# Full attention on one Trainium2 core: the product of weights and values in three one-pass products, and a query tile's maxima over both key halves at once

## The chip, the cores and the metric

One core of one Trainium2 chip runs the whole program. The metric is the time of one execution on the device, in microseconds (us); smaller is better. The program is written engine by engine: TensorE (PE; its weight loads are PEld), VectorE (DVE), ScalarE (ACT), GpSimd (POOL) and SyncE (SP) each run their own list of instructions in order, and semaphores tie them together.

## The reference, cut to what matters

The program is two transformer blocks. The change is in the attention of the first: 8 query heads and 2 key/value heads of width 64, over 1024 tokens, with no mask.

```
q, k, v = heads(q_a), heads(k_a), heads(v_a)      # 8, 2, 2 heads of 64
q = rope(rms_norm(q)); k = rope(rms_norm(k))
for each block of 128 queries:
    s = einsum('bkgqd,bksd->bkgqs', q, k) * 64 ** -0.5
    p = softmax(s, axis=-1)
    o = einsum('bkgqs,bksd->bkgqd', p, v)
```

All of it is in float32. The rest (projections, the bidirectional mLSTM, the feed-forward part, the second block with its banded and its forgetting attention) isn't touched.

## The kernel before, in words

A `Plan` lists steps; each engine then walks the same list and does its own part of every step. The order of that list is therefore the order on every engine. `attention` (L160) writes it for one kind of attention; "full" is the kind that the change touches.

**Jobs and units.** A job is one head and one half of the queries (512 queries): 16 jobs, numbered here 0 to 15. A job has 8 units, one for each tile of 128 keys. For unit g the plan puts down, in this order: the scores of the unit after it (`sc`); steps that are due (`mrow`, `take`, `div`, `qhi`, `qlo`); a unit of maxima for a later job (`max`); now and then a portion of other work for TensorE, `share` of one for each unit (9 matmuls, about, of the input projection, L1216 to L1218, or steps that prepare the mLSTM); and last the values of unit g (`val`).

**Scores.** `scores` (L1342, L1344) makes scores of 128 keys by 512 queries with keys along the partitions, in one of two PSUM banks (2 and 3). Each operand is split into a rounded part (type fp32r, which TensorE takes in one pass) and a low part (what the rounding left), so that two one-pass matmuls give the float32 product. The second of them (L1344) also subtracts the maximum of each query, through one extra row of `qa`.

**Weights and values.** ScalarE takes the exponential of the bank into `pf` (L1829, 128x512, float32), one of three buffers. `values` (L1366) multiplies `pf` by the values, both plain float32, into bank 6 or 7, where a job's 8 units add up. The stationary operand is 128 columns wide: 64 of values and 64 of ones, so rows 64 to 127 of the result hold the sums of the weights. A float32 matmul stands in the trace as two records. After a job's last unit `take` makes the reciprocals of the sums on ScalarE (a logarithm, L1837, and an exponential, L1839), and `divide` multiplies on VectorE (L2154, `y<-ps,rinv`).

**Maxima.** They have to be known before a job's first scores. `max_unit` computes one tile of 128 queries against one half of the keys (L1307, one matmul of 128x512), and VectorE takes the maximum of each row of the bank (L2290, 128x512). A job has 8 such units: 4 query tiles, 2 halves. VectorE then takes the larger of the two halves for all four tiles (`mx<-mh`, 128x4), four small matmuls with an identity turn the four columns into a row (`mrow`, L1323), and ScalarE copies that row into `qa` (L1809), which releases the semaphore `row`.

**The helper banks.** Banks 4 and 5 serve `max`, `mrow`, the turned values (`vprep`) and the turned gates, each step taking the other one than the step ahead of it. A step waits until the step two places before it has been emptied (`aux_emptied`): by VectorE's reduction (semaphore `aux`), or by ScalarE's copy of the row (`row`).

**Before the first scores** the plan has the maxima of job 0 and the first of job 1, two units of maxima and then a portion of projection matmuls in turn.

Of the kernel before, what the change touches and what calls it, by code (L numbers as in the profile page):

```python
# [15 lines left out]
P = 128  # L16
D = 1024
T = 1024
# [61 lines left out]
for _name, _n in (("b_ada", 48), ("b_ada_2", 24), ("norm_mix_g", 8), ("norm_ffn_g", 8),  # L80
# [16 lines left out]
    "half_mm y_out pad_made conv_taps conv_out m_kept m_in o_in rope_in qk_sq side_mm side_out qk_r qk_n qk_swap qk_cos qk_sin qk_rot "  # L97

    "at_set vt aux kk_hi kk_cp kk_lo q_hi q_cp q_lo mx_mm mcol rowt row sink_f sink_h sink_l sink_mm "
    "sc p_exp val ln_r inv div "  # L100
# [52 lines left out]
def max_units_of(kind, h, n):  # L153

    if kind == "band":
        return [(4 * n, None), (4 * n + 2, None)]
    return [(qt, half) for qt in range(4 * n, 4 * n + 4) for half in range(2) if kind == "full" or half <= n]


def attention(p, jobs, fill, share, at):  # L160
# [42 lines left out]
    for g, (i, u) in enumerate(units):  # L203
# [12 lines left out]
        if u == len(units_of(*job)) - 1:  # L216
            waiting.append(("take", *job))
# [492 lines left out]
def build(nc, a, out):  # L710
# [3 lines left out]
    with ExitStack() as ctx:  # L714
# [103 lines left out]
        class Buffers:  # L818
            def __init__(self, n, k_area, v_area, q_area, p_area):
# [4 lines left out]
                self.v = [v_area[i](f"{n}_v{i}", [P, KT, P], F32) for i in range(2)]  # L824
# [6 lines left out]
        A1 = Buffers("full", four(64, 72, 80, 88), four(68, 136), area, (76, 92, 144))  # L831
        A1.mx = [area(f"mx1_{i}", [P, 4], F32R) for i in range(3)]
        A1.mh = [area(f"mh1_{i}", [P, 2, 4], F32) for i in range(3)]
        area = Area(148, 152)
        A1.rinv = [area(f"rinv1_{i}", [64, HT], F32) for i in range(2)]
# [194 lines left out]

        def aux_bank(*step):
            return 4 + AUX_NO[step] % 2
# [5 lines left out]
        def aux_emptied(step):  # L1038

            i = AUX_NO[step] - 2  # L1040
            if i < 0:
                return None
            if AUX[i][0] == "gate":
                return s["g_cols"], G_COLS[AUX[i][1]]
            return (s["row"], no(*AUX[i])) if AUX[i][0] == "mrow" else (s["aux"], aux_no(*AUX[i]))
# [167 lines left out]
        def tensor(e):  # L1213
# [51 lines left out]
            def aux_free(step):  # L1265
                if emptied := aux_emptied(step):
                    e.wait_ge(*emptied)
# [9 lines left out]
            def max_unit(kind, h, n, u):  # L1277
# [26 lines left out]
                else:  # L1304
                    k0, k1 = half * HT, min((half + 1) * HT, T if kind == "full" else (qt + 1) * P)
                    if kind == "full":
                        x = e.matmul(ps[:, bank, 0:k1 - k0], q(qt), A.kk[kb][:, k0:k1], start=True, stop=True, skip_group_check=True)  # L1307
                    else:
# [1803 lines left out]
```

## Time and profile before

| what | value |
|---|---|
| median of 3 runs | 1998.36 us (1997.38 to 2002.4) |
| span of the profiled execution | 1999.4 us |
| TensorE busy in it | 1928.1 us (96%) |
| full attention, first scores to last values | about 278 to 519 us |
| granted TensorE clock there | 1.00 (of 2.4 GHz) |

The profile is one execution on the chip. A span of it is the time from its first instruction to its last; no other time of that execution is given, so the span stands for it. Busy times are unions of an engine's records. A record of ScalarE or VectorE can begin before the one ahead of it has ended, and so can TensorE's, whose ends are modelled; the distance from start to start is what an instruction costs in a dense stretch. "<-" behind an idle time names what ended it.

### The profile page before, as it was taken

How to read it: one execution, taken by the hardware profiler on the slowest of the kernel's cores; microseconds unless marked ns; L12 is line 12 of the kernel's file. 1: busy time of each engine (PE TensorE's matmuls, PEld its weight loads, DVE VectorE, ACT ScalarE, POOL GpSimd, SP SyncE). 2: the span in 40 equal slices, each digit the busy share in tenths (PEclk: the TensorE clock that was granted, in tenths of full speed). 3: DMA queues.
4: the chain of work that ended last, by engine and by line, in shares of the span. 5: the costliest groups of instructions: out<-in, count | busy, mean ns of one | idle time of the engine just before them, and what ended most of it. 6: DMA issues, size and time to landing. Idle time of an engine off the chain costs nothing.

```text
span 1999.4 us, 23686 instructions
## 1 busy us (share of the span) xinstructions
PE 1928.1 (96%) x8844; PEld 1507.4 (75%) x8844; DVE 1209.4 (60%) x1774; ACT 909.3 (45%) x1523; POOL 104.6 (5%) x188
## 2 busy tenths in 40 slices
PE   6999999999989989999999999999999999999888
PEld 4778876656787768888888788887888887776577
DVE  7794847655575687677555546556543555445744
ACT  5543345465553542333333435434523665445742
POOL 1101100000000000111000000000021000000000
PEclk9999999999999999999999999999999999999999
DMA  8437400010205423355221653333432001013062
GB/s 325 161 95 241 165 25 11 1 53 1 95 1 167 160 95 121 138 184 200 68 70 53 219 202 121 120 127 138 158 126 74 33 32 43 22 56 146 1 179 95
DMA packets 67151, 216.13 MB, mean 108 GB/s; under 512 B 8272, under 2 KB 13520, under 8 KB 66784
## 3 DMA queue, kind: packets, MB, share of 16 engines
q1 hardware_dynamic: 47168, 141.15, 21.1%
q0 software_dynamic: 19872, 73.48, 10.4%
q8 instruction: 72, 1.18, 0.2%
q14 instruction: 39, 0.32, 0.1%
HBM read 177.30 MB, written 34.61 MB: 106 GB/s over the span
## 4 chain that ended last, share of the span: by engine, by line
PE 57%; DVE 4%; ACT 2%; DMA 2%; issue 1%; DVEq 0%; SPq 0%; ACTq 0%
PE ps L1216 9%; PE ps L1218 8%; PE ps L1217 8%; PE ps L1522 6%; PE ps L1523 6%; PE ps L1524 6%; PE ps L1366 4%; DMA w_raw<-in_weights 2%; PE ps L1342 1%; PE ps L1344 1%; PE ps L1310 1%; DVE w_lo L2158 1%; PE ps L1652 1%; PE ps L1651 1%; PE ps L1650 1%
## 5 line engine op out<-in xcount | busy, mean ns | idle before, releaser
L1216 PE MATMUL ps<-h_hi,w_hi 128*128 128x512 f32 x832 | 335.5, 403 | 7.5 <-DVE h_lo L2158 5.2
L1218 PE MATMUL ps<-h_hi,w_lo 128*128 128x512 f32 x832 | 326.4, 392 | 0.0
L1217 PE MATMUL ps<-h_lo,w_hi 128*128 128x512 f32 x832 | 326.1, 392 | 0.0
L2158 DVE TENSOR_TENSOR w_lo<-w_raw,w_hi 128x1024 fp32r<-128x1024 f32 x139 | 170.0, 1224 | 244.0 <-ACT w_hi L1689 242.6
L1689 ACT ACTIVATE w_hi<-w_raw 128x1024 fp32r<-128x1024 f32 x140 | 147.6, 1056 | 243.6 <-DMA w_raw<-in_weights 241.8
L2290 DVE TENSOR_REDUCE mh<-ps 128x1 f32<-128x512 f32 (+1 forms) x224 | 140.2, 630 | 142.1 <-PE ps L1307 68.0
L1216 PEld LDWEIGHTS ps<-h_hi,w_hi 128*128 128x128 f32 x832 | 158.1, 190 | 43.1 <-DVE h_lo L2158 6.4
L1218 PEld LDWEIGHTS ps<-h_hi,w_lo 128*128 128x128 f32 x832 | 157.3, 189 | 34.1
L1217 PEld LDWEIGHTS ps<-h_lo,w_hi 128*128 128x128 f32 x832 | 157.7, 190 | 32.1 <-issue 1.4
L1216 PE MATMUL ps<-hid_hi,w_hi 128*128 128x512 f32 x352 | 138.1, 392 | 4.1 <-DVE hid_kept_lo L2158 1.9
L1522 PE MATMUL ps<-t_hi,pair_S_r 128*128 128x512 f32 x352 | 137.3, 390 | 4.4 <-DVE pair_S_r L2158 2.6
L1218 PE MATMUL ps<-hid_hi,w_lo 128*128 128x512 f32 x352 | 137.1, 389 | 0.0
L1524 PE MATMUL ps<-t_hi,pair_S_r 128*128 128x512 f32 x352 | 137.0, 389 | 0.0
L1523 PE MATMUL ps<-t_lo,pair_S_r 128*128 128x512 f32 x352 | 137.0, 389 | 0.0
L1366 PE MATMUL ps<-full_pf,full_v 128*128 128x512 f32 x256 | 131.0, 593 | 0.3 <-ACT full_pf L1829 0.2
L1829 ACT ACTIVATE second_pf<-ps 128x512 f32<-128x512 f32 (+2 forms) x128 | 65.1, 510 | 136.6 <-PE ps L1348 61.3
L1829 ACT ACTIVATE full_pf<-ps 128x512 f32<-128x512 f32 x128 | 76.1, 596 | 98.1 <-PE ps L1344 97.5
L1366 PE MATMUL ps<-second_pf,second_v 128*128 128x128 f32 (+3 forms) x336 | 111.8, 434 | 0.8 <-ACT second_pf L1829 0.7
L1342 PE MATMUL ps<-full_qq,full_kk 128*128 128x512 f32 x128 | 90.4, 706 | 0.2 <-issue 0.2
L1216 PE MATMUL ps<-mix_hi,w_hi 128*128 128x512 f32 x192 | 77.2, 402 | 8.8 <-ACT y_out L2121 6.1
L1342 PE MATMUL ps<-second_qq,second_kk 128*128 128x128 f32 (+3 forms) x168 | 83.5, 497 | 1.7 <-ACT second_pf L1829 0.7
L1216 PEld LDWEIGHTS ps<-hid_hi,w_hi 128*128 128x128 f32 x352 | 66.1, 188 | 20.5 <-DVE w_lo L2158 2.9
(405 smaller groups left out, 3829.9 us busy)
## 6 DMA issues: line engine op xcount, KB each, us to landing
w_raw<-in_weights SPq DMA_DIRECT2D x140, 512.0 KB, 3.6
ada_next<-in_ada POOLq DMA_DIRECT2D x32, 512.0 KB, 4.8
ada_last<-in_ada POOLq DMA_DIRECT2D x24, 512.0 KB, 5.2
pair_gate<-in_weights SPq DMA_DIRECT2D x22, 512.0 KB, 3.7
pair_up<-in_weights SPq DMA_DIRECT2D x22, 512.0 KB, 4.6
ada_first<-in_ada SPq DMA_DIRECT2D x8, 1024.0 KB, 17.7
m_scratch<-y POOLq DMA_DIRECT2D x12, 512.0 KB, 5.5
hid_scratch<-hid_out POOLq DMA_DIRECT2D x22, 256.0 KB, 2.3
```

The lines of the kernel that those rows point to most:

```text
L1216: e.matmul(o, w_hi[slot][:, tile_of(kw)], hi, start=start, stop=False, skip_group_check=skip)
L1217: e.matmul(o, w_hi[slot][:, tile_of(kw)], lo, start=False, stop=False, skip_group_check=skip)
L1218: return e.matmul(o, w_lo[slot][:, tile_of(kw)], hi, start=False, stop=stop, skip_group_check=skip)
L1342: e.matmul(o, A.kk[kb][:, keys], A.qq[b][:, q], start=True, stop=False, skip_group_check=True)
L1366: x = e.matmul(o, A.v[kb][:, kt, :], A.pf[p3][:, c:c + q1 - q0], start=(u == 0 and kind != "band"), stop=False, skip_group_check=True)
L1522: e.matmul(ps[:, bank, :], a_hi[:, tile_of(k)], b_hi[:, first + k, :], start=start and k == 0, stop=False, skip_group_check=True)
L1523: e.matmul(ps[:, bank, :], a_hi[:, tile_of(k)], b_lo[:, first + k, :], start=False, stop=False, skip_group_check=True)
L1524: x = e.matmul(ps[:, bank, :], a_lo[:, tile_of(k)], b_hi[:, first + k, :], start=False, stop=k == 3, skip_group_check=True)
L1689: return e.activation(dst, src, ACT.Copy)
L1829: e.activation(A.pf[p3][:, c0:c1], ps[:, bank, c0:c1], ACT.Exp, scale=SC).then_inc(s["p_exp"], 1)
L2158: return e.tensor_tensor(dst, src, hi.bitcast(F32), ALU.subtract)
L2290: x = e.tensor_reduce(A.mh[b][:, half, i:i + 1], ps[:, bank, 0:k1 - k0], AX_X, ALU.max)
```

## The change

For the full attention alone:

- **Weights times values.** ScalarE takes the exponential of a score bank twice: into `p_hi` (rounded, fp32r) and into `pf` (float32). VectorE subtracts one from the other into `p_lo` (step `plo`, in the place of `pf`). The values are split once for each key/value head into `v_hi` and `v_lo`. `values` is then `v_hi*p_hi` and `v_lo*p_hi` (the second with 64 stationary columns, since the ones have no low part), and a new step `vlo`, one unit later, adds `v_hi*p_lo`. The product of the two low parts is left out. `take` comes one unit later than before, and there is one `rinv` buffer where there were two.
- **Maxima.** A unit of maxima is a query tile against all 1024 keys: two matmuls into banks 4 and 5, then one reduction over 128x1024 straight into `mx`. A job has 4 such units; from job 3 on they stand at every other unit of the plan. VectorE's combination of halves is gone, and `mrow` on TensorE waits for the reductions themselves. A maxima step waits until both banks have been emptied.
- Semaphores of the rotary part are joined into one (`qk_step`) with the same order of instructions.

```diff
@@ max_units_of
+    if kind == "full":
+        return [(qt, None) for qt in range(4 * n, 4 * n + 4)]
@@ attention
-        low = max(first[i - 2], high - len(maxima) + 1) if i >= 3 else high - len(maxima) + 1
+        span = 2 * len(maxima) if jobs[i][0] == "full" and i >= 3 else len(maxima)
+        low = max(first[i - 2], high - span + 1) if i >= 3 else high - span + 1
...
+        if job[0] == "full":
+            p.add("plo", *job, u)
         for step in rows + waiting + others + slots.get(g, []):
             p.add(*step)
...
         p.add("val", *job, u)
...
+        if job[0] == "full":
+            if g:
+                p.add("vlo", *jobs[units[g - 1][0]], units[g - 1][1])
@@ buffers
+        A1.rinv = [Area(148, 150)("rinv1", [64, HT], F32)] * 2
+        A1.p_hi = [Area(start, start + 2)(f"full_p_hi{i}", [P, HT], F32R) for i, start in enumerate((94, 146, 150))]
+        A1.p_lo = [Area(start, start + 2)(f"full_p_lo{i}", [P, HT], F32R) for i, start in enumerate((76, 92, 144))]
@@ helper banks
+            banks = (4, 5) if x[:2] == ("max", "full") else (4 + AUX_NO[x] % 2,)
@@ aux_emptied
-            i = AUX_NO[step] - 2
...
+            for b in AUX_BANKS[step]:
+                i = AUX_USED[b].index(step) - 1
@@ TensorE, max_unit
+                        for n1 in range(2):
+                            x = e.matmul(ps[:, 4 + n1, :], q(qt), A.kk[kb][:, half_of(n1)], start=True, stop=True, skip_group_check=True)
@@ TensorE, values and values_low
+                if kind == "full":
+                    e.matmul(ps[:, bank, :], A.v_hi[kb][:, u, :], A.p_hi[p3][:, :], start=u == 0, stop=False, skip_group_check=True)
+                    e.matmul(ps[0:64, bank, :], A.v_lo[kb][:, u, :], A.p_hi[p3][:, :], start=False, stop=False,
+                             skip_group_check=True).then_inc(s["val_hi"], 1)
+                    return
...
+                e.wait_ge(s["p_lo"], i)
+                e.matmul(ps[:, 6 + job_no(kind, h, n) % 2, :], A.v_hi[kb][:, u, :], A.p_lo[(i - 1) % 3][:, :], start=False,
+                         stop=False, skip_group_check=True).then_inc(s["val"], 1)
@@ ScalarE, scores
+                if kind == "full":
+                    if i > 3:
+                        e.wait_ge(s["val_hi"], i - 3)
+                        e.wait_ge(s["p_lo"], i - 3)
...
+                    e.activation(A.p_hi[p3][:, :], ps[:, bank, :], ACT.Exp, scale=SC).then_inc(s["p_hi"], 1)
@@ VectorE, max_unit
+                elif kind == "full":
+                    x = e.tensor_reduce(A.mx[b][:, i:i + 1], flat(4), AX_X, ALU.max)
@@ VectorE, p_low
+                e.wait_ge(s["p_exp"], i)
+                low_part(A.p_lo[p3][:, :], A.pf[p3][:, :], A.p_hi[p3][:, :]).then_inc(s["p_lo"], 1)
```

TensorE where one job hands over to the next but one (the row of job 10's maxima is turned, and the maxima of job 11 begin). `full_qq,full_kk` and `full_qa,full_ka` are the two matmuls of the scores, `full_kk,full_qq` the maxima, `ident_r,mx` the turned row. Before:

```order
L1344 MATMUL ps<-full_qa_142,full_ka_138 128x512
L1323 MATMUL ps<-ident_r,mx_1_151 1x128 [waits ident_made,mcol,aux]
L1323 MATMUL ps<-ident_r,mx_1_151 1x128 x3
L1307 MATMUL ps<-full_kk_136,full_qq_141 128x512 [waits q_cp,kk_lo,q_hi,aux]
L1366 MATMUL ps<-full_pf_147,full_v_146 128x512 [waits p_exp]
L1342 MATMUL ps<-full_qq_140,full_kk_136 128x512 [waits kk_lo,kk_cp,q_lo,at_set,row,p_exp]
L1344 MATMUL ps<-full_qa_143,full_ka_138 128x512
L1307 MATMUL ps<-full_kk_136,full_qq_141 128x512 [waits kk_lo,row]
```

And of the changed program:

```order
L1372 MATMUL ps<-full_qa_142,full_ka_138 128x512
L1351 MATMUL ps<-ident_r,mx_1_149 1x128 [waits ident_made,aux]
L1351 MATMUL ps<-ident_r,mx_1_149 1x128 x3
L1331 MATMUL ps<-full_kk_136,full_qq_141 128x512 [waits q_cp,kk_lo,q_hi,row,aux]
L1331 MATMUL ps<-full_kk_136,full_qq_141 128x512
L1393 MATMUL ps<-full_p_hi_152,full_v_hi_159 128x512 [waits p_hi]
L1394 MATMUL ps<-full_p_hi_152,full_v_lo_161 64x512
L1406 MATMUL ps<-full_p_lo_157,full_v_hi_159 128x512 [waits p_lo]
L1370 MATMUL ps<-full_qq_140,full_kk_136 128x512 [waits kk_lo,kk_cp,q_lo,at_set,row,p_exp]
```

The wait for `row` stood at the scores after the values (L1342) and now stands at the maxima right behind the turned row (L1331), ahead of the values. The same pair stands so at the rows of jobs 2 to 14, 13 times.

ScalarE at the same kind of place, where the row is copied. In the changed program:

```order
L1876 ACTIVATE full_p_hi_154<-ps 128x512 [waits p_lo,val_hi,sc]
L1879 ACTIVATE full_pf_147<-ps 128x512 [waits val]
L1854 ACTIVATE full_qa_142<-ps 1x512 [waits sc,rowt]
L1876 ACTIVATE full_p_hi_152<-ps 128x512 [waits p_lo,val_hi,sc]
L1879 ACTIVATE full_pf_145<-ps 128x512 [waits val]
L1728 ACTIVATE full_qq_141<-y 64x512 [waits qk_rot,sc]
```

Ahead of the copy (L1854) stand two exponentials of the newest scores, where there was one (L1829).

## Rows read from the trace of the kernel before

**Rows 1.** The page, busy time of each engine over the span.

```profile
PE 1928.1 (96%) x8844; PEld 1507.4 (75%) x8844; DVE 1209.4 (60%) x1774; ACT 909.3 (45%) x1523; POOL 104.6 (5%) x188
```

**Rows 2.** Stretches of jobs 1 to 4, of job 4 alone, of job 8: us, busy by engine, clock.

```profile
297.50:359.83 62.33, 62.19 (x225) 39.57 (x223) 47.01 (x65) 34.62 (x58) 0.00 (x0) 1.00 0.03 9
343.31:359.83 16.52, 16.38 (x62) 10.57 (x60) 14.05 (x23) 10.65 (x18) 0.00 (x0) 1.00 0.00 0
405.28:418.24 12.96, 12.96 (x47) 7.68 (x45) 7.63 (x14) 7.21 (x13) 0.00 (x0) 1.00 0.53 201
```

**Rows 3.** Timeline of TensorE in the last job: start, us, engine, line, operation.

```profile
512.03 0.39 PE L1344 MATMUL ps<-full_qa,full_ka 65*128 65x512 f32 x1
512.26 1.02 PE L1366 MATMUL ps<-full_pf,full_v 128*128 128x512 f32 x2
...
513.35 0.40 PE L1344 MATMUL ps<-full_qa,full_ka 65*128 65x512 f32 x1
513.59 0.59 PE L1366 MATMUL ps<-full_pf,full_v 128*128 128x512 f32 x1
```

**Rows 4.** Groups by line and form, 275 to 522 us: count, busy, mean ns, idle before.

```profile
L2290 DVE TENSOR_REDUCE mh<-ps 128x1 f32<-128x512 f32 x120 | 82.2, 687 | 66.4 <-PE ps L1307 65.8
L1829 ACT ACTIVATE full_pf<-ps 128x512 f32<-128x512 f32 x128 | 76.1, 596 | 98.1 <-PE ps L1344 97.5
L1323 PE MATMUL ps<-ident_r,mx 128*1 128x128 f32 x64 | 6.5, 223 | 3.6 <-issue 2.4 <-DVE mh L2290 1.0
```

**Rows 5.** Timeline of all engines where job 8 hands over.

```profile
413.57 0.40 PE L1344 MATMUL ps<-full_qa,full_ka 65*128 65x512 f32 x1
413.81 0.40 PE L1323 MATMUL ps<-ident_r,mx 128*1 128x128 f32 x4
414.00 0.60 ACT L1829 ACTIVATE full_pf<-ps 128x512 f32<-128x512 f32 x1 [0.96 <-PE ps L1344]
414.05 0.44 PE L1307 MATMUL ps<-full_kk,full_qq 128*128 128x512 f32 x1
414.33 1.02 PE L1366 MATMUL ps<-full_pf,full_v 128*128 128x512 f32 x2
...
414.63 0.58 ACT L1809 ACTIVATE full_qa<-ps 1x512 fp32r<-1x512 f32 x1
...
415.28 0.19 PEld L1342 LDWEIGHTS ps<-full_qq,full_kk 128*128 128x128 f32 x1 [0.76 <-ACT full_pf L1829]
```

**Rows 6.** Timeline of ScalarE, two exponentials without a wait between.

```profile
434.89 1.06 ACT L1829 ACTIVATE full_pf<-ps 128x512 f32<-128x512 f32 x2
```

**Rows 7.** Timeline of ScalarE at a take.

```profile
431.22 0.59 ACT L1837 ACTIVATE rinv<-ps 64x512 f32<-64x512 f32 x1
431.84 0.63 ACT L1839 ACTIVATE rinv<-rinv 64x512 f32<-64x512 f32 x1
432.50 0.60 ACT L1829 ACTIVATE full_pf<-ps 128x512 f32<-128x512 f32 x1
```

**Rows 8.** Groups of VectorE by form, whole span.

```profile
L2158 DVE TENSOR_TENSOR w_lo<-w_raw,w_hi 128x1024 fp32r<-128x1024 f32 x139 | 170.0, 1224 | 244.0 <-ACT w_hi L1689 242.6
...
L2290 DVE TENSOR_REDUCE mh<-ps 128x1 f32<-128x384 f32 x16 | 8.9, 556 | 5.9 <-PE ps L1313 5.7
...
L2290 DVE TENSOR_REDUCE mh<-ps 128x1 f32<-128x128 f32 x16 | 4.7, 291 | 14.2 <-PE ps L1313 14.2
```

**Rows 9.** Timeline of projection matmuls, and of the first maxima.

```profile
257.04 0.39 PE L1216 MATMUL ps<-h_hi,w_hi 128*128 128x512 f32 x1
...
257.72 0.39 PE L1216 MATMUL ps<-h_hi,w_hi 128*128 128x512 f32 x1
...
264.52 0.61 PE L1307 MATMUL ps<-full_kk,full_qq 128*128 128x512 f32 x2
...
265.89 1.28 DVE L2290 TENSOR_REDUCE mh<-ps 128x1 f32<-128x512 f32 x2
```

More of the change, by code:

```diff
@@ L156, in max_units_of @@
         return [(4 * n, None), (4 * n + 2, None)]
-    return [(qt, half) for qt in range(4 * n, 4 * n + 4) for half in range(2) if kind == "full" or half <= n]
+    if kind == "full":
+        return [(qt, None) for qt in range(4 * n, 4 * n + 4)]
+    return [(qt, half) for qt in range(4 * n, 4 * n + 4) for half in range(2) if half <= n]
 def attention(p, jobs, fill, share, at):
@@ L215, in attention @@
         p.add("val", *job, u)
-        if u == len(units_of(*job)) - 1:
-            waiting.append(("take", *job))
+        ended = (g, i, u)
+        if job[0] == "full":
+            if g:
+                p.add("vlo", *jobs[units[g - 1][0]], units[g - 1][1])
+            if g == len(units) - 1:
+                p.add("vlo", *job, u)
+            else:
+                ended = (g - 1, *units[g - 1]) if g else None
+        if ended and ended[2] == len(units_of(*jobs[ended[1]])) - 1:
+            waiting.append(("take", *jobs[ended[1]]))
     while fill:
@@ L1029, in build @@
         AUX_NO = {x: i for i, x in enumerate(AUX)}
+        AUX_USED, AUX_BANKS = {4: [], 5: []}, {}
+        for x in AUX:
+            banks = (4, 5) if x[:2] == ("max", "full") else (4 + AUX_NO[x] % 2,)
+            AUX_BANKS[x] = banks
+            for b in banks:
+                AUX_USED[b].append(x)
         def aux_bank(*step):
-            return 4 + AUX_NO[step] % 2
+            return AUX_BANKS[step][0]
         def aux_no(*step):
@@ L1265, in aux_free @@
             def aux_free(step):
-                if emptied := aux_emptied(step):
+                for emptied in aux_emptied(step):
                     e.wait_ge(*emptied)
@@ L1304, in max_unit @@
                 else:
-                    k0, k1 = half * HT, min((half + 1) * HT, T if kind == "full" else (qt + 1) * P)
                     if kind == "full":
-                        x = e.matmul(ps[:, bank, 0:k1 - k0], q(qt), A.kk[kb][:, k0:k1], start=True, stop=True, skip_group_check=True)
+                        e.wait_ge(s["kk_lo"], no("klo", kind, kb, 1))
+                        for n1 in range(2):
+                            x = e.matmul(ps[:, 4 + n1, :], q(qt), A.kk[kb][:, half_of(n1)], start=True, stop=True, skip_group_check=True)
                     else:
+                        k0, k1 = half * HT, min((half + 1) * HT, (qt + 1) * P)
                         diagonal = k1 == (qt + 1) * P
@@ L1353, in values @@
                 p3, bank = (i - 1) % 3, 6 + job % 2
-                e.wait_ge(s["p_exp"], i)
+                e.wait_ge(*((s["p_hi"], i) if kind == "full" else (s["p_exp"], i)))
                 if u == 0:
@@ L1761, in head_squares @@
                 if r >= 2:
-                    e.wait_ge(s["qk_n"], r - 1)
+                    e.wait_ge(s["qk_step"], 4 * (r - 2) + 1)
                 e.wait_ge(s["y_out"], no("y1", t, 1))
@@ L1834, in take @@
                 e.wait_ge(s["val"], no("val", kind, h, n, last_unit((kind, h, n))))
-                if job >= 2:
-                    e.wait_ge(s["div"], job - 1)
-                e.activation(rinv[:, :], ps[64:P, bank, :], ACT.Ln).then_inc(s["ln_r"], 1)
-                e.wait_ge(s["ln_r"], job + 1)
+                if job >= 1:
+                    e.wait_ge(s["div"], job if kind == "full" else job - 1)
+                e.activation(rinv[:, :], ps[64:P, bank, :], ACT.Ln).then_inc(s["inv"], 1)
+                e.wait_ge(s["inv"], 2 * job + 1)
                 e.activation(rinv[:, :], rinv[:, :], ACT.Exp, scale=-1.0).then_inc(s["inv"], 1)
```

76 lines of the change are left out of this document (46 added, 30 removed).

## The prediction

> **What bounds the kernel now.** I read the page first, then busy time by stretch, then the timeline where jobs meet. TensorE is busy for 96% of the span, no other engine for more than 60% [rows 1]. The full attention says the same: in job 8, which has no other work mixed in, TensorE is busy for all 12.96 us, VectorE for 7.63, ScalarE for 7.21 [rows 2]. So what TensorE issues is paid in full, and the other two engines have some 5 us of room in a job. The question is how much of that room the change eats, and in which order the three now wait for each other.
>
> **Products of weights and values.** In the last job, without maxima, a unit takes 1.33 us (512.26 to 513.59), and the second score matmul takes 0.24 of it (513.35 to 513.59) [rows 3]. With two one-pass matmuls of about 0.235, the float32 product is left with 0.86 us. Three one-pass products at 0.235 take 0.705, which is 0.155 less, over 128 units 19.8 us. The nearest other price is the projection's pace, 0.68 us for three (257.04 to 257.72) [rows 9]; with it the gain would be 23. I take 0.235, since the new matmuls wait and signal as those of the scores do. The 64-column load isn't in the trace; nothing says that a shorter load shortens a pass by more than the projection's pace shows.
>
> For a 512-column matmul the Trainium skill (TensorE: Matmul & The Clock Gate, Back-to-back issue gap) gives 512/2.4 + 2.5, about 216 ns. The float32 product agrees (0.86 for four passes); the one-pass matmuls don't. By its figure alone the gain would be 27.6 us, an estimate.
>
> **The wait for the turned row, the largest new cost.** Maxima now take both helper banks. In the order of the changed program, 13 times (jobs 2 to 14), the pair of maxima stands right behind the turned row and waits until ScalarE has copied that row. Before, the maxima took the other bank and the value product (0.86 us) stood between; the wait was met almost exactly [rows 5]: second score matmul 413.57, turned row 413.81, free for the next at 414.05; the exponential begins at 414.00, 0.43 after 413.57; the copy at 414.63, 0.63 later; it ends at 415.21, and the next scores load at 415.28.
> In the changed order two exponentials stand ahead of the copy. A second one follows its like by 0.48 (1.06 less 0.58) [rows 6]. So the copy ends 0.43 + 0.48 + 0.63 + 0.58 = 2.12 after the second score matmul, the maxima start at about 2.17, and TensorE was ready at 0.48: **1.69 us idle, 13 times, 22.0 us**. Bounds: 20 if the copy too follows by 0.48, 24 if the exponentials are 0.62 apart. Behind the waiting pair stand the values of the unit, its low product, portions of projection and the next job's first scores, so nothing fills the hole. For the rows of jobs 1 and 15 no maxima follow; the next job's first scores wait, behind 0.7 us of products: together 1.5 us (0 to 2).
>
> The Trainium skill (Perfetto Trace Analysis, Matmuls) wants independent matmul groups to rotate through PSUM banks, so that one is emptied while the next is computed. The change gives that up for the maxima.
>
> **Waits that go.** TensorE's turned row used to wait for the last reduction and the combination of halves, 3.6 us in all [rows 4]; the last pair now stands two units ahead of it. The short wait there (the product of 414.33 would have let the scores start at 415.19; they start near 415.31) [rows 5] is replaced too, 15 times 0.12. Together -5.4 us (-3.6 to -5.4).
>
> **ScalarE.** It gains 128 exponentials of 0.60 us [rows 4], 0.48 apart at the least: 8 x 0.48 = 3.8 to 8 x 0.62 = 5.0 us a job on 7.2 busy [rows 2], in a job of some 13. That fits, except at the take: logarithm and exponential are 0.62 apart and the next exponential follows 0.66 later [rows 7]. Counted from the second score matmul of that unit, the next `p_hi` starts at 0.91 + 0.62 + 0.62 + 0.66 = 2.81 and is done at 3.41; TensorE, after 13 more passes of 0.235, wants it at 3.05. That is 0.4 us a job where no other work stands in that unit; I count 10 of 16 jobs, 4 us (0 to 7).
>
> **VectorE.** A job gains 8 subtractions, 0.60 us each when dense (128x512, by the pace of the reductions: 1.28 for two [rows 9]), 4.8 us. Its 8 reductions of 0.687 [rows 4] become 4 over 1024 columns. From 128 to 384 columns a reduction grows from 291 to 556 ns, 1.04 ns a column; that gives 687 + 530 = 1.22 us, as a 1024-column subtraction takes (1224 ns) [rows 8]. So -0.6, and 0.2 for the combination: **+4.0 us a job**. Job 8: 11.6 of 12.96 - 1.24 + 1.69 = 13.4, enough. Jobs 1 to 4, where the gates' scans run: 47.0 + 16 = 63.0 us of work against 62.3 - 5.0 + 3 x 1.69 + 1 = 63.4 of TensorE, waits included [rows 2]. Even on average, so bursts spill over: job 4 has 14.05 + 4.0 = 18.1 against 16.5 - 1.2 + 1.7 = 17.0. I take 3 us (0 to 8, if nothing is evened out and the mLSTM's preparation in jobs 11 to 15 is held up too). The waits for the row give VectorE time to catch up; without them this would be the bound.
>
> **Ahead of and behind the stage.** The plan begins with two pairs of maxima in a row. The second waits for the first reduction, which can't begin before 265.89 [rows 9]: idle from about 265.0 to 267.2. The fourth waits for the third likewise, about 1.3. Before, banks alternated, and about 1 us was lost there. Net +2.5 us (0 to 3.5). At the end the last low product waits for exponential, exponential, subtraction: +0.6 (0 to 1). The rotary semaphores move no instruction: 0, since each is waited for by the next on the same engine.
>
> **The sum.** -19.8 + 22.0 + 1.5 - 5.4 + 4 + 3 + 2.5 + 0.6 = +8.4 us. The profiled span is 1.0 above the median of the runs, so I add to the median: 1998.4 + 8.4 = **2006.8 us**. Later stages are bound by TensorE as well, and move by as much.
>
> **Rivals.**
> *The passes run faster and the other engines keep up* (the side of a gain). One mechanism: the new matmuls reach the projection's pace, which gives 3.3 us more, and projection work falls into the units of the takes and bursts, so the 4 and the 3 aren't paid. Then 2006.8 - 3.3 - 7 = 1996.5, and with the copy 0.48 behind the exponential (-1.8) and half of the start 1993.5. For it: the projection [rows 9]. Against: every one-pass matmul beside a semaphore in this stage is 0.235 apart. A gain beyond the noise begins where this and the lower bound of the row's wait come together. 11%.
> *The passes run at 0.216.* 0.019 us less for each of 384 products is 7.3 us: 1999.5, no change. The float32 passes do run at that pace [rows 3]; against it, no one-pass matmul here does. The Trainium skill (same page and section) would have it so. 12%.
> *ScalarE becomes the bound.* If both exponentials and what follows are 0.62 apart, a job asks for 16 x 0.62 + 2.5 = 12.4 us, and between the copied row and the next scores ScalarE is idle for 1.9: 14.3 against 13.8 with the take, and more in jobs with the mLSTM's work. 8 us more: 2015. The take [rows 7] speaks for 0.62, the pair of exponentials [rows 6] against. 12%.
> *The wait for the row doesn't bite*, because something fills it: excluded by TensorE's order, in which all behind the pair waits too. It would be 1985; 1%, within the first.
> The forecast has the remaining 65%.
>
> **Numbers.** A measurement of this kernel can tell about 0.3%, 6 us, from no change: 1992.4 and 2004.4 are the bounds. The forecast with its bounds lies above 2004.4 for some 52 of its 65%, within for 13. Slower: 52 + 12 = 64%. Same: 13 + 12 = 25%. Faster: 11%. All lower bounds together give 1990, all upper ones 2020; 8 times in 10 it should be between 1995 and 2016.
>
> **What would show it.** Right: 13 idle times of TensorE of about 1.7 us in the full attention, ended by ScalarE's copy of the row (L1854); three products of a unit in about 0.7 us; TensorE's busy time in the stage down by about 20 us and its idle time up by more; reductions of 1.2 us; VectorE near full in jobs 1 to 4. Wrong: idle times at the maxima under 1 us, products 0.65 us or 0.8 us a unit, idle times at `p_hi` or `p_lo` that outweigh those at the row, or a difference outside the stage (278 to 519 us now).

## The result, and the profile after

The changed kernel takes **2034.78 us**, the median of four runs (2033.52 to 2038.76), against 1999.77 for four runs of the kernel before beside them (1997.38 to 2002.4): a ratio of 1.0177, 95% interval 1.0161 to 1.0193. It is 35 us slower. The forecast was 2006.8 us, 8.4 more than before, with a range of 1995 to 2016. The sign was right, the size was not.

The page of the changed kernel, busy time over the span of 2033.4 us (beside [rows 1]):

```profile
PE 1919.2 (94%) x8972; PEld 1524.7 (75%) x8972; DVE 1276.7 (63%) x1822; ACT 970.5 (48%) x1653; POOL 104.2 (5%) x188
```

TensorE is busy for 8.9 us less and the span is 34.0 us longer, so TensorE waits. The stretches of jobs 1, 2, 4, 6, 7 and 8, from one take to the next (beside [rows 2]): start and end, length, then busy time of PE, PEld, DVE, ACT and POOL, and PE's granted clock.

```profile
302.09:322.21 20.12, 16.86 (x72) 11.67 (x70) 15.89 (x18) 12.26 (x22) 0.00 (x0) 1.00 0.00 1
322.21:343.03 20.82, 16.83 (x63) 12.18 (x63) 15.72 (x19) 10.88 (x21) 0.00 (x0) 0.84 0.00 0
...
360.22:381.33 21.11, 16.58 (x70) 11.49 (x69) 19.28 (x26) 15.51 (x27) 0.00 (x0) 1.00 0.00 0
...
397.91:421.18 23.27, 19.99 (x102) 14.62 (x101) 13.17 (x18) 13.13 (x26) 0.00 (x0) 1.00 0.00 1
421.18:439.00 17.82, 14.12 (x62) 10.24 (x61) 11.52 (x16) 12.47 (x24) 0.00 (x0) 0.90 0.02 3
439.00:452.95 13.95, 12.21 (x54) 8.50 (x54) 11.54 (x16) 10.94 (x21) 0.00 (x0) 1.00 0.46 184
```

Lengths of the jobs, worked out from the starts of the takes' logarithms (L1837 before, L1887 after; job 0 from 264.00, "rest" from the last take to the end of the span):

| | before | after | more |
|---|---|---|---|
| job 0 | 33.5 | 38.1 | 4.6 |
| jobs 1 to 4 | 62.3 | 79.2 | 16.9 |
| jobs 5 to 7 | 45.5 | 57.7 | 12.2 |
| jobs 8 and 9 | 25.9 | 27.8 | 1.9 |
| jobs 10 to 15 | 88.4 | 89.7 | 1.3 |
| rest | 1479.8 | 1476.9 | -2.9 |

So jobs 8 and 9, which have no other work in them, pay 0.9 us each, and the loss lies in jobs 0 to 7. Two things shift the borders: a take now comes one unit later, so that the row of job 0 holds a unit more (1.2 us or more) and that of jobs 10 to 15 one less; and the first maxima began at 265.36 in this run, at 264.52 in the run of the kernel before. From the first maxima to the last take the stage is 36.0 us longer. TensorE's groups there and behind, 278 to 560 us (count, busy, mean ns, idle before and what ended it):

```profile
L1393 PE MATMUL ps<-full_p_hi,full_v_hi 128*128 128x512 f32 x128 | 51.9, 405 | 5.4 <-ACT full_p_hi L1876 5.2
L1406 PE MATMUL ps<-full_p_lo,full_v_hi 128*128 128x512 f32 x128 | 51.8, 405 | 6.4 <-DVE full_p_lo L2208 6.3
...
L1331 PE MATMUL ps<-full_kk,full_qq 128*128 128x512 f32 x120 | 41.0, 423 | 27.7 <-ACT full_qa L1854 14.0 <-issue 7.9 <-DVE mx L2341 4.9
...
L1417 PE MATMUL ps<-ident,g_f_log 64*128 64x64 f32 x8 | 0.7, 229 | 2.1 <-DVE mx L2341 2.1
```

L1331 is the pair of maxima, L1393 and L1406 the first and the low product, L1417 gate transposes that use the maxima's banks. Pauses by single rows add up thus: 13 times a pair waits 1.2 to 2.4 us for the turned row's copy (8 rows "full_qa", 5 "issue", 21.9 us), 9 times a low product for VectorE's subtraction (6.4), 7 times a pair for a reduction (4.9), twice a gate transpose for a reduction (3.0), 9 times a first product for ScalarE (5.4). A pass is booked for 0.40 us though the next may start 0.235 after it, so each pause of one pass after another is some 0.16 us longer than its idle time. The same holds behind a turned row, whose passes of 128 columns follow by 0.06 us: the 13 pauses come to 24.1 us.

The forecast hand-over, at the end of job 8, all engines:

```profile
444.96 0.40 PE L1372 MATMUL ps<-full_qa,full_ka 65*128 65x512 f32 x1
...
445.20 0.41 PE L1351 MATMUL ps<-ident_r,mx 128*1 128x128 f32 x4
...
445.40 0.60 ACT L1876 ACTIVATE full_p_hi<-ps 128x512 fp32r<-128x512 f32 x1
445.89 0.59 ACT L1879 ACTIVATE full_pf<-ps 128x512 f32<-128x512 f32 x1
446.51 0.58 ACT L1854 ACTIVATE full_qa<-ps 1x512 fp32r<-1x512 f32 x1
...
447.14 0.50 PE L1331 MATMUL ps<-full_kk,full_qq 128*128 128x512 f32 x1 [1.54 <-ACT full_qa L1854]
```

It went as worked out: the copy L1854 ends 2.13 after the second score matmul (2.12 forecast), the pair starts at 2.18 (2.17). TensorE was ready at 0.49, so this pause is 1.69 us, though 1.54 are booked. From 443.56 to 444.73 a unit without maxima takes 1.17 us where one took 1.33 [rows 3], that is 0.16 less (0.155 forecast).

What was not forecast, in job 2:

```profile
325.92 2.28 DVE L2379 TENSOR_TENSOR_SCAN g_f_log<-g_f_log,g_zeros 32x1024 f32<-32x1024 f32 x1
...
326.76 0.39 PE L1394 MATMUL ps<-full_p_hi,full_v_lo 128*64 128x512 f32 x1
328.23 1.29 DVE L2208 TENSOR_TENSOR full_p_lo<-full_pf,full_p_hi 128x512 fp32r<-128x512 f32 x2
...
328.98 0.50 PE L1406 MATMUL ps<-full_p_lo,full_v_hi 128*128 128x512 f32 x1 [1.83 <-DVE full_p_lo L2208]
...
329.44 1.22 DVE L2341 TENSOR_REDUCE mx<-ps 128x1 fp32r<-128x1024 f32 x1
...
329.79 0.51 PE L1393 MATMUL ps<-full_p_hi,full_v_hi 128*128 128x512 f32 x1
...
330.10 0.63 PE L1394 MATMUL ps<-full_p_hi,full_v_lo 128*64 128x512 f32 x1
...
330.53 0.63 PE L1406 MATMUL ps<-full_p_lo,full_v_hi 128*128 128x512 f32 x1
...
330.95 0.63 PE L1370 MATMUL ps<-full_qq,full_kk 128*128 128x512 f32 x1
```

A gate scan holds VectorE until 328.20, two subtractions follow, and the low product stands for 1.83 us. Soon after, at 329.9, the passes last 0.63 us and follow each other by 0.43: the granted clock is 1.2 instead of 2.4 GHz. In stretches of 4 us, TensorE's busy time and clock:

```profile
264.00:268.00 4.00, 1.98 (x9) 1.00 0.01 2
268.00:272.00 4.00, 3.92 (x10) 0.57 0.00 0
...
324.00:328.00 4.00, 3.15 (x13) 1.00 0.00 0
328.00:332.00 4.00, 3.02 (x10) 0.74 0.00 0
332.00:336.00 4.00, 2.64 (x10) 0.50 0.00 0
...
421.00:425.00 4.00, 1.89 (x14) 1.00 0.00 0
425.00:429.00 4.00, 4.00 (x13) 0.57 0.00 0
```

Three times in the stage TensorE had stood for half of 4 us (264 and 421) or had paused again and again (324), and then ran at half clock for some us. Pauses of 2.30 and 2.35 us (ended at 477.36 and 525.61) brought no fall. The kernel before shows 1.00 in all its jobs; its one fall between 40 and 1800 us lies behind the stage, at 688.65, where the changed kernel has none. To count this in every run I use what each run lists, its span and its mean granted clock: the span times (1 - clock) is the **clock loss**, the span times the clock the **full-clock span** (the clock is listed to 0.001, 2 us in one run, less in a mean of several). Means over the runs: before 1985.3 to 1986.3 us full-clock span and 11.7 to 13.6 us of loss in four sets of 7 to 23 runs; after 2014.8 and 18.8. So of the 35 us, 29 are waits and work, 5 to 7 the clock. The split is approximate, since the full-clock span varies within one kernel too (1982.1 to 1990.3 in 19 runs of the kernel before): in a mean of four runs, differences of 2 us say little.

### The profile page after: what moved, and what is told of

Same layout as the page of the kernel before. It is cut to its first block, busy times and chain, and to the rows that moved or that the text cites. A ratio compares the mean times of both kernels' runs of the same rounds, so it can differ in the third digit from the quotient of the medians.

```text
span 2033.4 us, 24118 instructions
## 1 busy us (share of the span) xinstructions
PE 1919.2 (94%) x8972; PEld 1524.7 (75%) x8972; DVE 1276.7 (63%) x1822; ACT 970.5 (48%) x1653; POOL 104.2 (5%) x188
## 3 DMA queue, kind: packets, MB, share of 16 engines
q1 hardware_dynamic: 47168, 141.15, 19.8%
## 4 chain that ended last, share of the span: by engine, by line
PE 79%; DVE 10%; ACT 5%; issue 3%; DMA 3%; SPq 0%; DVEq 0%; ACTq 0%
PE ps L1239 13%; PE ps L1241 13%; PE ps L1240 13%; PE ps L1561 6%; PE ps L1563 6%; PE ps L1562 6%; PE ps L1399 4%; PE ps L1370 2%; DMA w_raw<-in_weights 2%; PE ps L1372 2%; DVE mx L2341 1%; PE ps L1331 1%; DVE w_lo L2208 1%; PE ps L1335 1%; PE ps L1406 1%
## 5 line engine op out<-in xcount | busy, mean ns | idle before, releaser
L1876 ACT ACTIVATE full_p_hi<-ps 128x512 fp32r<-128x512 f32 x128 | 76.6, 599 | 71.7 <-PE ps L1372 69.9
L2208 DVE TENSOR_TENSOR full_p_lo<-full_pf,full_p_hi 128x512 fp32r<-128x512 f32 x128 | 85.9, 684 | 28.1 <-ACT full_pf L1879 26.9
L2341 DVE TENSOR_REDUCE mx<-ps 128x1 fp32r<-128x1024 f32 x64 | 77.9, 1217 | 34.8 <-PE ps L1331 34.6
L2344 DVE TENSOR_REDUCE mh<-ps 128x1 f32<-128x512 f32 (+2 forms) x96 | 52.9, 555 | 73.5 <-PE ps L1335 39.0
```

The costliest lines, as they stand in the source:

```text
L1876: e.activation(A.p_hi[p3][:, :], ps[:, bank, :], ACT.Exp, scale=SC).then_inc(s["p_hi"], 1)
L2208: return e.tensor_tensor(dst, src, hi.bitcast(F32), ALU.subtract)
L2341: x = e.tensor_reduce(A.mx[b][:, i:i + 1], flat(4), AX_X, ALU.max)
```

## Experiments

All ratios are to the kernel before on the same chip, with 95% intervals.

| kernel | median us | ratio | full-clock span | clock loss |
|---|---|---|---|---|
| values_only | 2015.74 | 1.0086 (1.0069 to 1.0103) | 1993.5 | 21.1 |
| maxima_only | 2020.93 | 1.0109 (1.0094 to 1.0124) | 2003.1 | 16.2 |
| row_early | 2027.87 | 1.0141 (1.0124 to 1.0158) | 2002.9 | 23.3 |
| no_subtract | 2027.03 | 1.0143 (1.0124 to 1.0163) | 2006.3 | 19.8 |
| values_comb_first | 2010.27 | 1.0049 (1.0032 to 1.0066) | 1990.1 | 18.1 |
| row_before_scores | 2022.13 | 1.0112 (1.0097 to 1.0127) | 1999.5 | 21.2 |
| no_sub_row_early | 2011.30 | 1.0061 (1.0045 to 1.0077) | 1992.3 | 18.1 |
| waits_filled | 2035.32 | 1.0178 (1.0157 to 1.0199) | 2019.0 | 14.8 |
| maxima_earlier | 2009.04 | 1.0042 (1.0028 to 1.0057) | 1991.4 | 16.1 |
| low_first | 2005.91 | 1.0019 (1.0008 to 1.0030) | 1987.2 | 16.0 |
| low_first_nosub | 1998.04 | 0.9991 (0.9978 to 1.0004) | 1981.7 | 14.5 |
| split_second_key | 1999.92 | 0.9999 (0.9986 to 1.0011) | 1983.6 | 15.2 |

### values_only: the products alone

```diff
-    if kind == "full":
-        return [(qt, None) for qt in range(4 * n, 4 * n + 4)]
+    return [(qt, half) ... for half in range(2) if kind == "full" or half <= n]
```
with banks in turn, one reduction a half and the combination on VectorE, as in the kernel before.

> The values in three one-pass products as in the change, the maxima as before it (eight halves, banks in turn, halves combined on VectorE). Theory A (the loss is the pair of banks: 13 waits for the turned row, and a pair that waits for its own reduction, each made worse by VectorE being late): no idle time of TensorE behind the row, -19.8 for the products, +4 at the takes, +4 to +8 where VectorE is overloaded in jobs 1 to 4 (11.7 + 4.8 us of work in a job of some 14.5): 1988 to 1994 us. Theory B (VectorE's and ScalarE's added work alone makes the loss beyond the 22 us of the row waits): 2034.8 - 22 = about 2013 us, with TensorE's clock falling as in the changed kernel.

Measured 2015.7, above both and 3 us from B. Theory A had overlooked an order. VectorE and TensorE where job 10 hands over:

```profile
456.01 0.68 DVE L2202 TENSOR_TENSOR full_p_lo<-full_pf,full_p_hi 128x512 fp32r<-128x512 f32 x1
...
456.60 0.15 DVE L2198 TENSOR_TENSOR mx<-mh 128x4 fp32r<-128x4 f32 x1
...
456.86 0.40 PE L1345 MATMUL ps<-ident_r,mx 128*1 128x128 f32 x4 [1.62 <-issue]
```

The combination of the halves (456.60) stands behind a subtraction, which waits for the second exponential; so the turned row waits 1.62 us. Over 16 rows the idle time is 16.0 us (14 rows wait, 0.6 to 2.5 us each), near the 17.6 us lost.

### maxima_only: the maxima alone

The kernel before, with the change's plan, banks and reductions of the maxima; values in float32.

> The maxima of the change (pairs over both banks, one reduction), the values in float32 as before. Behind the turned row one exponential less stands ahead of the copy: the copy ends 0.43 + 0.63 + 0.58 = 1.64 us after the second score matmul, so 13 waits of 1.2 us, 15.8 us; waits gone -5.4, start +2.5; VectorE has less to do than before, so by theory A and B alike no more than 1 or 2 us of other waits and the clock stays at 1.00 behind the start: 2009 to 2014 us. If the single pair of banks is costly by itself (a pair waits for its reduction with VectorE idle too), 2020 us or more.

Measured 2020.9, the number put down for a pair of banks that is costly by itself, but only in part for that reason; the full-clock span is 17.5 above that of the kernel before, where 12.9 were expected.

```profile
L1320 PE MATMUL ps<-full_kk,full_qq 128*128 128x512 f32 x128 | 42.2, 411 | 18.8 <-ACT full_qa L1825 8.9 <-issue 5.5 <-DVE mx L2305 4.0
```

The waits for the copy are there, 8.9 + 5.5 = 14.4 us in 13 (15.8 forecast). The other 4.0 are waits for reductions, 3.5 of them at the start; two gate transposes wait 0.5 each besides. So with VectorE below its old load the single pair of banks costs some 2 us behind the start by itself, beside the waits for the copy. The clock takes 4.5 us more than in the kernel before. Half of the change, without the added exponentials and subtractions, is thus slower than the kernel before by 23 us, and the other half by 18: together 40, where the whole is 35 slower.

### row_early and row_before_scores: the turned row moved

```diff
-        at_unit.setdefault(first[i] - 2, []).append(("mrow", *job))
+        at_unit.setdefault(first[i] - (3 if job[0] == "full" and i >= 3 else 2), []).append(("mrow", *job))
```

> The changed kernel with the turned row of jobs 3 to 15 one unit earlier, in a unit without maxima, so that its copy is done when the next pair comes. If the 1.54 us idle times at the pair are the wait for the copy, 12 of 13 go and at most 0.35 us comes in their place (the row now waits for its last reduction): 2034.8 - 12 x 1.69 + 12 x 0.35 = 2018.7 us at most of the gain kept, down to 2014. If VectorE is the bound of jobs 3 to 7, the waits there are only moved to the subtractions and reductions, and the gain is half: 2025 us.

In row_before_scores a full job's `mrow` is added to the plan ahead of `("sc", ...)` instead of behind it.

> The changed kernel with the turned row of every full job ahead of the next unit's scores instead of behind them, so that ScalarE copies it ahead of both exponentials. The copy then ends about 0.43 + 0.58 + 0.24 = 1.25 us after the row begins, TensorE reaches the pair after 0.71: 0.55 us idle instead of 1.69, 13 times, 14.8 us less: 2020 us. If the row is then late itself (its last reduction, VectorE behind in jobs 3 to 7) or the clock falls more often, up to 2028.

Measured 2027.9 and 2022.1. The first missed both of its numbers, 2014 to 2019 and 2025; the second lies in its range. The full-clock spans fell by 12.0 and 15.4 us, where 16 and 14.8 were expected; the clock took back 4.5 and 2.4. In row_early:

```profile
L1331 PE MATMUL ps<-full_kk,full_qq 128*128 128x512 f32 x128 | 43.9, 425 | 11.6 <-DVE mx L2341 8.5 <-ACT full_qa L1854 1.6 <-DVE full_v_lo L2208 0.8
...
L1351 PE MATMUL ps<-ident_r,mx 128*1 128x128 f32 x64 | 6.6, 228 | 6.1 <-DVE mx L2341 6.0
```

The waits for the copy (L1331, full_qa) fell from 21.9 to 1.6, and in their place the row (L1351) waits 6.0 for its last reduction and the pairs 8.5 for theirs. Both runs say that the row wait was worth what it was put down for, with a part given back.

### no_subtract and no_sub_row_early: VectorE relieved

```diff
-                e.wait_ge(s["p_lo"], i)
-                e.matmul(..., A.v_hi[kb][:, u, :], A.p_lo[(i - 1) % 3][:, :], ...)
+                e.wait_ge(s["p_exp"], i)
+                e.matmul(..., A.v_hi[kb][:, u, :], A.p_hi[(i - 1) % 3][:, :], ...)
```
and `p_low` on VectorE returns at once. ScalarE's rounded exponential waits for this product three units back in place of the subtraction; TensorE's order has it done before the scores that the exponential takes anyway.

> The changed kernel without VectorE's subtraction; the third product takes the rounded weights a second time in place of the low part (so the weights' low part is left out of the result), all passes and both exponentials stay. Theory A and B: VectorE's queue is what keeps maxima, low products and gate transposes waiting (about 14 us in jobs 0 to 7) and these waits are what halves TensorE's clock (6.6 us): 2034.8 - 20 = 2012 to 2018 us, row waits still 1.54 us x 13, granted clock 1.00 from 278 on. Rival (the loss is in the order of the program and ScalarE): 2030 us or more.

> The changed kernel with both: no subtraction on VectorE (third product with the rounded weights, so their low part is left out of the result) and the turned row one unit earlier. With each profile's loss at half clock taken off its span, row_early stands 14.0 us and no_subtract 13.9 us below the changed kernel. If row waits and VectorE's load are separate causes the two add: span less loss 1989 us, measured 2000 to 2008 with 11 to 18 us of loss. If they are one cause (VectorE sets both), about 2000 less loss, measured 2012 or more.

no_subtract measured 2027.0, between its two numbers: it gave 8.5 us of full-clock span where about 14 were expected, and no clock where 6.6 were. The waits for the subtraction are gone, but the pair's are not:

```profile
L1393 PE MATMUL ps<-full_p_hi,full_v_hi 128*128 128x512 f32 x128 | 52.3, 409 | 5.8 <-ACT full_p_hi L1875 5.7
...
L1331 PE MATMUL ps<-full_kk,full_qq 128*128 128x512 f32 x128 | 43.6, 423 | 29.5 <-ACT full_qa L1854 13.5 <-issue 7.9 <-DVE mx L2340 7.2
```

Of 7.2 us of waiting for reductions (DVE mx) 3.5 lie at the start; the rest stayed with VectorE relieved by 4.8 us a job. The two long ones and a gate transpose (2.1) wait for a reduction that stands behind the division of the job just ended (`y<-ps,rinv`, at 301.69 and 409.61) or behind gate instructions (at 365.8 and 367.3), whatever the average load.

With both edits the time is 2011.3, between the 2008 of two causes and the 2012 of one. The full-clock span decides: it is 22.5 us shorter, where the single edits give 12.0 + 8.5 = 20.5 and one cause would give 12 to 14. The row wait and VectorE's load are separate causes, and add.

### values_comb_first, maxima_earlier, low_first: VectorE's order

values_comb_first is values_only with `plo` added to the plan behind `mrow` instead of ahead of it.

> Values in three one-pass products, maxima as before the change, and on VectorE the combination of the halves placed ahead of the subtraction of that unit instead of behind it. In values_only the row waited 1.62 us for a combination (456.60) that stood behind the subtraction (456.01), 16 us in all. Theory (a matter of order alone): these 16 us fall to the 3.6 of the kernel before: 2015.7 - 12.4 = 2003 us, 2000 if TensorE's clock falls less often too. Rival (VectorE's and ScalarE's load is the bound, and the waits only move to p_hi and p_lo): 2010 us or more.

```diff
-        high = min(first[i] - 3, end)
+        high = min(first[i] - (4 if jobs[i][0] == "full" and i >= 3 else 3), end)
```

> values_comb_first with the maxima of jobs 3 to 15 one unit earlier, so that the last reduction and the combination are done when the row comes. In values_comb_first TensorE still stood idle 9.1 us ahead of the row; its span times its granted clock is 1990.1, against 1985.9 for the kernel before, and it lost 18.1 us to the clock against 12.0. Theory (waits and clock are what is left between the two, the work itself is 20 us less): 7 us of idle time go, span times clock 1983, measured 1998 to 2003, the lower end if the clock falls less often. Rival (VectorE is the bound in jobs 1 to 4, so the wait turns up at p_lo or the maxima): 2008 to 2011, no change from values_comb_first.

low_first also adds `plo` at the head of a unit, ahead of the gates' steps, and the combination right behind the last maximum.

> As maxima_earlier, with two steps of VectorE's order changed besides: a unit's subtraction stands ahead of the gate scans of that unit instead of behind them, and the combination right behind the last reduction. Theory (the 5.4 us that TensorE waits for p_lo are bursts in VectorE's order): they fall to 1 or 2 us, 4 us less than maxima_earlier: 1994 to 1999. Rival (VectorE's average load in jobs 1 to 4 is over TensorE's): the wait moves to the maxima and the time is that of maxima_earlier.

Measured 2010.3, 2009.0 and 2005.9. The first had its rival's number: the row's wait fell from 16.0 to 9.1 us, not to 3.6, and the next scores waited 3.1 where they had waited 0.8. The second changed nothing, as its rival said, but the wait stayed at the row (9.1 again), where the combination had kept its place in VectorE's list. The third lies between its two numbers, and it makes two moves at once. The groups of maxima_earlier and then of low_first:

```profile
L1330 PE MATMUL ps<-full_kk,full_qq 128*128 128x512 f32 x128 | 51.8, 410 | 1.4 <-DVE mh L2338 1.1
...
L1402 PE MATMUL ps<-full_p_lo,full_v_hi 128*128 128x512 f32 x128 | 51.4, 402 | 4.7 <-DVE full_p_lo L2204 4.7
...
L1347 PE MATMUL ps<-ident_r,mx 128*1 128x128 f32 x64 | 6.4, 223 | 9.1 <-issue 4.7 <-DVE mh L2338 4.1
```

```profile
L1332 PE MATMUL ps<-full_kk,full_qq 128*128 128x512 f32 x128 | 52.0, 412 | 8.6 <-DVE mh L2340 8.2
...
L1404 PE MATMUL ps<-full_p_lo,full_v_hi 128*128 128x512 f32 x128 | 50.4, 394 | 0.2 <-DVE full_p_lo L2206 0.2
```

The low product's wait fell from 4.7 to 0.2 us and the row's from 9.1 to nothing that shows, and the maxima's rose from 1.4 to 8.6. Jobs 2 and 5 of low_first, columns as above, show why: VectorE is busy for 18.64 of 18.83 and 17.70 of 17.99 us (over jobs 2 to 5 for 67.7 of 69.4, TensorE for 61.0). Order only chooses who waits.

```profile
313.42:332.25 18.83, 17.77 (x76) 13.06 (x77) 18.64 (x28) 12.32 (x22) 0.00 (x0) 1.00 0.00 0
...
364.78:382.77 17.99, 16.65 (x75) 12.48 (x76) 17.70 (x31) 11.60 (x21) 0.00 (x0) 1.00 0.00 1
```

The same kernel in a job without gates, the unit from 421.50 on, TensorE alone:

```profile
421.50 0.40 PE L1368 MATMUL ps<-full_qq,full_kk 128*128 128x512 f32 x1
...
422.21 0.39 PE L1391 MATMUL ps<-full_p_hi,full_v_hi 128*128 128x512 f32 x1
...
422.90 0.40 PE L1368 MATMUL ps<-full_qq,full_kk 128*128 128x512 f32 x1
```

Six passes in 1.40 us, 0.17 less than before. Eight such units would save 1.3 us, but job 8 takes 12.60 where it took 12.96. The other 1.0 us goes at the hand-over to three short pauses: 0.4 at the first product after the take, 0.2 at the row's successor, and 0.4 at the next job's scores, which start 0.1 after the end of a copy (419.36 to 419.94) that stands behind two exponentials.

### low_first_nosub and split_second_key: the end of the argument

> low_first without VectorE's subtraction (third product with the rounded weights, so their low part is left out of the result). In low_first TensorE waits 8.2 us for reductions where it had waited 5.4 for p_lo before. Theory (VectorE's amount of work in jobs 1 to 4 is the bound there, not its order): these 8 us go, span times clock 1987 - 8 = 1979, and with fewer waits the clock falls less often: 1990 to 1995 us, below the kernel before. Rival (the waits come from ScalarE's second exponential and from the order of the plan): 2003 us or more.

In split_second_key heads 0 to 3 keep `A.v` in float32 and the one matmul; `plo`, `vlo`, `p_hi` and `v_hi` exist for heads 4 to 7 alone.

> A mixture: heads 0 to 3 (jobs 0 to 7, in whose time the gates' scans run on VectorE) with the float32 product as before the change, heads 4 to 7 (jobs 8 to 15) with the three one-pass products; maxima of single halves, in low_first's order. Where VectorE has room the products give 8 x 1.24 = 9.9 us, the takes give back 8 x 0.4 = 3.2, the row's 3.6 us of waiting go: span times clock 1985.3 - 10.3 = 1975, and with the clock's loss of the kernel before (12 to 14 us) 1988 to 1991 us, faster than both kernels. Rival (even there the waits of TensorE that the change brings halve the clock more often): 1995 to 2000 us, the same as before.

Measured 1998.0 and 1999.9, both the same as the kernel before (0.9978 to 1.0004, and 0.9986 to 1.0011), both missing what the theory expected; the second has the number of its rival. Without the subtraction the waits for maxima fell:

```profile
L1368 PE MATMUL ps<-full_qq,full_kk 128*128 128x512 f32 x128 | 53.9, 421 | 8.7 <-issue 5.2 <-ACT full_pf L1876 3.1 <-ACT full_qa L1852 0.4
L1332 PE MATMUL ps<-full_kk,full_qq 128*128 128x512 f32 x128 | 51.7, 409 | 1.7 <-DVE mh L2339 1.7
L1391 PE MATMUL ps<-full_p_hi,full_v_hi 128*128 128x512 f32 x128 | 51.5, 402 | 5.5 <-ACT full_p_hi L1873 5.2
```

from 8.6 to 1.7 us, and the full-clock span by 5.5: VectorE's amount of work was the bound there. But 8.7 us of waiting show ahead of the scores (L1368; 5.2 in low_first) and 5.5 at the first product (5.1): some of them for ScalarE's exponentials and copies (3.5 and 5.2), and 5.2 put down to nothing that the profile shows. split_second_key has a full-clock span 2 us under the kernel before instead of 10. Its job 9 takes 12.62 against 12.98, so a job saves far less than 1.24 (job 8, 13.98 against 12.96, holds nine units, since the takes come a unit later from there on). Jobs 8 to 15 together take 113.9 against 114.3, with two falls of the clock among them. Jobs 0 to 7, which have the old products, end 3.4 us later; 1.6 of that was there when the stage began (first maxima at 266.07 against 264.52), and the rest no run here explains. The rival's clock is borne out in part: the loss is 2.5 us above that of the kernel before. No version beats the kernel before.

### waits_filled: does idle time bring the clock down?

```diff
+                    for _ in range(idle):
+                        e.matmul(ps[:, spare, :], q(qt), A.kk[kb][:, half_of(0)], start=True, stop=True, skip_group_check=True)
                     aux_free(("max", kind, h, n, u))
```
with `idle` 6 behind a turned row, 9 and 6 at two maxima of job 0, into a bank that nobody uses then.

> The changed kernel with passes that compute nothing of use put into TensorE's waits: 6 in each of the 13 waits behind the turned row (6 x 0.233 = 1.40 of 1.69 us), 9 and 6 in the two waits of the first maxima. Theory C (TensorE's clock falls because TensorE stands idle): no fall at 268, and fewer in jobs 3 to 8; the time is the same or up to 5 us shorter, 2030 to 2035 us, though 93 passes (22 us of TensorE's work) are added. Rival (the falls have another cause, or the passes do not fit the holes): as many falls at half clock as in the changed kernel, 2035 us or more.

Measured 2035.3, as the changed kernel, with 93 passes more, at the border between the two expectations. The profiled run, in stretches of 4 us:

```profile
268.00:272.00 4.00, 4.00 (x19) 1.00 0.00 0
...
332.00:336.00 4.00, 3.91 (x18) 1.00 0.00 0
...
420.00:424.00 4.00, 2.01 (x14) 1.00 0.00 0
424.00:428.00 4.00, 4.00 (x21) 1.00 0.01 2
```

None of the three falls of the stage is left in it, though at 420 TensorE still stands for half of the stretch. But the mean loss over its four runs is 14.8 us against 18.8: two ran at a clock of 0.995 and 0.996, two at 0.990, no better than the changed kernel. Two runs of four thus speak for idle time as what brings the falls, and two don't: it is likely, not shown. What decides whether a given pause brings one stays open. The profiled run of low_first has pauses of up to 2.05 us in the stage and no fall there; its falls beyond those of the kernel before lie behind the stage, at 580, 737, 1122 and 1887 us, in a part that no version changed. So a loss above that of the kernel before can't all be put down to the pauses of the stage.

## Why the prediction was wrong, point by point

By its own terms, in the order of the sum. The right column is what TensorE's pauses from 264 us on add up to, each counted from the start of the pass before it less 0.233 us (0.06 behind a turned row).

| term | forecast | found |
|---|---|---|
| products | -19.8 | -20 (0.16 to 0.17 a unit) |
| wait for the turned row | +22.0 | +24.1 (13, 1.85 on average) |
| waits that go | -5.4 | -6.6 |
| take, ScalarE | +4 (0 to 7) | +6.9 |
| VectorE | +3 (0 to 8) | +19 |
| start | +2.5 (0 to 3.5) | +2.6 |
| TensorE's clock | none | +6.8 |
| rows of jobs 1 and 15, end | +2.1 | about +1 |

These make 33.8 of the 36.0 us by which the stage of the profiled run is longer; 2.2 stay unassigned. The rest of the program took 2.9 us less, 1.7 of it for the fall at 688.65 that only the kernel before had.

**Right:** what bounds the kernel, the products, the wait for the turned row (13 times; in the clean case to 0.01 us, over the stage 24.1 against 22.0, the upper bound given), the reduction (1.22 us) and the start. The Trainium skill (TensorE: Matmul & The Clock Gate, Back-to-back issue gap), whose 216 ns would have saved 7.3 us more, is not borne out for these passes: 0.23 to 0.235 again. The Trainium skill (Perfetto Trace Analysis, Matmuls) wants independent groups to rotate through banks. maxima_only agrees: giving it up brought 14.4 us of waits behind the turned row.

**The step that failed: "I take 3 us (0 to 8...)" for VectorE.** It set the sums of work over jobs 1 to 4 side by side, 63.0 against 63.4 us, and concluded that bursts would just spill over. The sum for VectorE was nearly right: it was busy 65.6 us in those jobs, which took 79.2. But the waits came to 19 us, since a burst in one unit isn't made good in the next: low products wait 7.9 us, pairs 6.1, gate transposes 3.6 (the prediction did not name them as users of these banks), others 1.4. Before three of the low products (4.3 us) stands a gate scan of 2.3 us, before three more (2.7) other gate instructions. Before one pair and two of the transposes (5.1) stands the division of the job just ended. no_subtract shows 8.5 us going with the load, low_first_nosub 5.5, and low_first shows waits moving from one place to another. The 9.7 us at pairs and transposes need both halves of the change: with banks in turn and all the added work (values_only) 1.8 us stand there, with the single pair of banks and less work (maxima_only) 2.3 behind the start. The price of this meeting had no term in the sum.

**ScalarE's term** was right in kind and short in size, 6.9 against 4. A third of it is one wait (2.4 us, ended at 470.62) behind the take and two instructions of the mLSTM's preparation of 1.04 us each.

**The sentence that misled:** "The waits for the row give VectorE time to catch up". no_sub_row_early speaks against it: the row wait and VectorE's load add instead of covering each other.

**Put at nothing: the clock.** The kernel before shows 1.00 through the stage, so its trace had no row for what pauses do to it. The changed kernel lost 6.8 us by it in the stage. Every variant lost more on average than the kernel before (14.5 to 23.3 us against 11.7 to 13.6), and row_early and row_before_scores gave back 4.5 and 2.4 us of their gain that way. The Trainium skill (TensorE: Matmul & The Clock Gate, A second HAM failure mode: psum-queue depth-cycling) describes a clock that goes back and forth where TensorE pauses briefly and often between groups of matmuls that cycle through banks. The three falls in the stage, after pauses of at most 2.1 us, agree; that the banks have to do with it no run here shows.

**The rivals.** Against a gain stand the passes, 0.23 to 0.235 apart in this kernel too, and the waits that did come. ScalarE as the bound would have given 2015, nearer to the result, but for the wrong reason: ScalarE cost 6.9 us, and its pace at the hand-over (0.49 and 0.62 apart) is the forecast's. The direction came out for the stated reason, the row's wait (24.1) outweighing the products (-20). What the forecast lacked is most of VectorE's 19 us and the clock's 6.8.

## What to carry to other kernels

A ratio of sums is no test for an engine that comes second: if the first engine can run ahead by one or two units only, lay the second engine's long or late instructions (here a scan of 2.3 us, and a division that waits for ScalarE) into one unit and see who stands behind them. Cheaper arithmetic on the bounding engine is worth what the hand-overs leave of it: here 1.3 us a job came to 0.4 in low_first, since two of the three pauses of each hand-over lie behind doubled exponentials. And where TensorE has had no pauses and will get some, add a term for the clock: the versions here lost 2 to 12 us more than the kernel before.

## What the runs showed of the hardware

- Passes at half clock are booked at 0.63 us and follow by 0.43, against 0.40 and 0.23. A fall in the changed kernel's stage lasted 3.4 us (from 268.5 and from 425.5) or 6.8 (from 329.9), and came after idle times of no more than 2.1 us.
- The falls vary from run to run of one kernel: waits_filled ran at 0.990 and at 0.996, low_first at 0.989 to 0.995, with 2008.6 and 1999.3 us of span. The kernel before varies too (0.991 to 0.996). In low_first's twelve runs the span varies by 9.4 us, the full-clock span by 5.3.
- A weight load of 64 columns (booked at 137 ns, one of 128 at 190) is no help to the pace: in jobs 8 and 9 the next pass follows by 0.23 us, as behind the others. One reduction over 1024 columns in two banks takes 1.22 us, where two over 512 take 0.69 each.
